# Block 2's gate and up projections in pairs of tiles by seven half-size products

## The chip, the cores and the metric

The kernel runs on one core of a Trainium2 chip. The metric is the device time of one execution in microseconds (us). All work is in float32. Matrix products that matter are made from float32r operands: each operand is split into a high half (rounded to float32r) and a low half (what is left), and three matmuls (high by high, high by low, low by high) are added in PSUM.

## The reference

Two transformer blocks of depth 2 on 512 tokens of width 1024. The part that the change touches is the feed-forward network of the second block, in both of its layers; it reads the whole token matrix `h` (512 x 1024):

```python
D_FF_2 = -(-(8 * D_MODEL) // (3 * 256)) * 256          # 2816
...
        h = h + mix @ w_out[l]
        hn = rms_norm_2(h, ffn_norm[l])
        gu = hn @ w_gate_up[l]
        h = h + (jax.nn.silu(gu[..., :D_FF_2]) * gu[..., D_FF_2:]) @ w_down[l]
```

## The kernel before

Activations lie feature-major: 128 features on the partitions, 512 tokens (`S`) in the free direction, so the width of 1024 is 8 k-tiles (`KD`) and the hidden width of 2816 is 22 tiles (`KF`). Weights come from HBM as units of 128 x 1024 float32 (512 KB): one unit holds the 8 k-tiles of one output tile. A ring of 4 units (`RING`) is filled by DMAs that SyncE issues (L425); a slot is filled again when `unit_free` says that its unit was split. For each unit ScalarE writes the high half into one of 2 slots (`SPLIT`) of `w_high` (L450) once TensorE is done with the unit two before (`split_used`), VectorE writes the low half into `w_low` (L453), and TensorE then does 8 k-tiles x 3 matmuls with it (L488), each 128x128 weights against 128x512 tokens.

The gate/up stage of block 2 has 22 output tiles of 2 units (gate, up). The tile's two products stand in banks 0 and 2 (or 4 and 6) of PSUM. The norm comes late: its gain is in the operand, and the reciprocal root of the mean square per token, `inv_rms`, is found during tile 0 (`LateNorm`: mean matmuls L560 on TensorE, root L1070 on ScalarE, three chained operations on VectorE, L783 to L785) and multiplied in when PSUM is read. Per tile (class `Swiglu`, scaled form): VectorE scales the gate (L1817) and the up part (L1818), ScalarE applies SiLU (L1801), VectorE multiplies (L1823), and the hidden tile is split for the down projection, high by ScalarE (L1789), low by VectorE (L1795), one tile later.

The down projection has 8 output tiles of 3 units (22 k-tiles). Its tile is added to the residual stream by VectorE (L1763), and the next norm's operand and squares are made tile by tile (L1024, L1029, L539). Its tile 0 waits for each hidden tile's halves, k by k.

Each engine's instructions are written out by hand in the order of its queue; semaphores alone tie the engines together. Nothing is planned by costs. `split_ahead` puts the next tile's unit splits ahead of the eviction of this tile on ScalarE and VectorE. `wait_tile` waits until the matmuls of a tile are done.

Of the kernel before, what the change touches and what calls it, by code (L numbers as in the profile page):

```python
# [22 lines left out]
ALU = mybir.AluOpType  # L23
# [21 lines left out]
RING = 4  # L45
SPLIT = 2
ADA_COLS = 256


Z_KA, Z_VA, Z_KB, Z_VB, Z_QA, Z_QB, Z_GA, Z_GB = 0, 1, 2, 3, 4, 8, 12, 20  # L50
# [19 lines left out]
def col_units(w):  # L70

    k, n = w.shape
    kt = k // P
    u = w.reshape(kt, P, n // P, P).transpose(2, 1, 0, 3).reshape(n // P, P, kt * P)
    pad = -u.shape[2] % UNIT
    if pad:
        u = np.concatenate([u, np.zeros((u.shape[0], P, pad), np.float32)], axis=2)
    return u.reshape(n // P, P, -1, UNIT).transpose(0, 2, 1, 3).reshape(-1, P, UNIT)


def modulation_units(w):
# [50 lines left out]
def weight_stream(a):  # L132
    out = []
    order = head_order()
    for l in range(DEPTH):
        qa, ka, va, qb, kb, vb, ga, gb = np.split(a["w_in"][l], np.cumsum([512, 128, 128, 512, 128, 128, D]), axis=1)
        keys, queries = pair_order(2), order[pair_order(8)]
        out.append(col_units(np.concatenate([ka[:, keys], va, kb[:, keys], vb, qa[:, queries], qb[:, queries], ga, gb], axis=1)))
        out.append(col_units(np.concatenate([a["w_proj_a"][l][order], a["w_proj_b"][l][order]], axis=0)))
        out.append(col_units(a["w_out"][l]))  # L140
        gate, up = col_units(a["w_ffn_gate"][l]), col_units(a["w_ffn_up"][l])
        out.append(np.stack([gate, up], axis=1).reshape(-1, P, UNIT))
        out.append(col_units(a["w_ffn_down"][l]))
    for l in range(DEPTH):
        w = a["w_in_2"][l]
        rope = np.concatenate([rope_order(w[:, 2560:], g) for g in range(4)], axis=1)
        out.append(col_units(np.concatenate([shift_order(w), w[:, SHIFTED * P:1920], rope, w[:, 1920:2560]], axis=1)))
        q_up = a["mla_w_q_up_2"][l].reshape(Q_RANK, HEADS, NOPE + ROPE)
        q_up = np.concatenate([rope_order(q_up[:, h, NOPE:], g) for g, h in enumerate(ROPE_HEADS)] +
                              [q_up[:, h, :NOPE] for h in range(HEADS)], axis=1)  # L150
        for k in range(Q_RANK // P):
            out.append(unit_of([(0, q_up[k * P:k * P + P])]))
        kv = a["mla_w_kv_up_2"][l].reshape(KV_RANK, HEADS, 2, HD)
        for part in range(2):
            m = kv[:, :, part].reshape(KV_RANK, HEADS * HD)
            out.append(unit_of([(0, m[:P]), (0, m[P:])]))
        out.append(col_units(a["w_out_2"][l]))
        gate, up = col_units(a["w_gate_up_2"][l][:, :DFF]), col_units(a["w_gate_up_2"][l][:, DFF:])
        out.append(np.stack([gate, up], axis=1).reshape(-1, P, UNIT))
        out.append(col_units(a["w_down_2"][l]))  # L160
    return np.concatenate(out)

# [145 lines left out]
def build(nc, dram, where, where1, where2, where3, n_units):  # L308
    with ExitStack() as ctx:
# [99 lines left out]
        def bank(n, w=BANK):  # L409
            return ps[:, n * BANK:n * BANK + w]  # L410
# [173 lines left out]
        def split_hidden(where_to):  # L584
# [17 lines left out]
            if where_to == "context":  # L602
                spans = [low[:, n:n + S] for n in range(KD * S, KD * T, S)]
                after = len(spans)
                spans += [m[:, n * S:n * S + S] for m, w in ((high, KD * T // S), (low, KD)) for n in range(w)]
            else:
                spans = [m[:, n * S:n * S + S] for m, w in ((high, KD * T // S), (low, KD)) for n in range(w)]
                spans += [low[:, n:n + S] for n in range(KD * S + 4 * C, KD * T, S)]
                after = KF
            return [[(hidL[:, k, :], spans[k], arena_r[:, k * S:k * S + S])] for k in range(KF)], after  # L610


# [1131 lines left out]
        class Residual(Evict):  # L1744


            def __init__(self, gate, later=None):
                self.gate, self.later = gate, later

            def scalar(self, act, g, t, c):  # L1750
                act.wait_ge(left_v.sem, left_v.at(t + 1))
# [6 lines left out]
            def vector(self, dve, g, t, c):  # L1758
                wait_tile(dve, g, t)
                for s, w in g.segs:  # L1760
                    x = (xL, xC)[s][:, t, :]
                    gate = 1.0 if self.gate is None else mod[:, self.gate + t, s:s + 1]
                    ins = dve.scalar_tensor_tensor(x, bank(4 * (c % 2) + s, w), gate, x, ALU.mult, ALU.add)  # L1763
                ins.then_inc(left_v.sem, 1)
                if self.later and t:
# [92 lines left out]
                        c.base += KF  # L1858

        gate_scaled, silu_out, hidden_out = (count(n) for n in ("gate_scaled", "silu_out", "hidden_out"))  # L1860
        first_root = arena[:, 21 * S:22 * S]

        def gemm(tiles, body, units, parts, segs, split, on_scalar=False):
# [1145 lines left out]
        for l in range(DEPTH):  # L3009
# [2 lines left out]
            mla(l)  # L3012
            inner_norm = late_norm("ffn", l, spare)
            next_norm = late_norm("attn", l + 1, spare) if l + 1 < DEPTH else None
            halves, after = split_hidden("alone")
            operand = [[(None, z2_r[:, HEADS + k if k < 4 else 2 * (k - 4), :], loL[:, k, :])] for k in range(KD)]
            stages = [Stage([gemm(KD, 4, 1, K8, segments(False), operand)], Residual(None, inner_norm), made=True)]
            stages += mlp(False, None, inner_norm, halves, after, None, next_norm)
# [49 lines left out]
```

## Time and profile before

| | |
|---|---|
| timed runs (3) | 3495.92, 3497.52, 3500.83 us; median 3497.52 |
| profiled execution, span | 3496.1 us |
| PE (TensorE matmul) busy | 3352.0 us, 96% |
| PEld (TensorE weight load) busy | 2656.6 us, 76% |
| DVE (VectorE) busy | 1643.4 us, 47% |
| ACT (ScalarE) busy | 1223.3 us, 35% |
| POOL (GpSimd) busy | 423.3 us, 12% |
| DMA | 82 GB/s in the mean |

Busy shares are means over the whole span. Rows of the trace give a start in us from the span's start, a duration, and behind them in brackets how long the engine sat idle before and which operation released it. A matmul's duration there is its latency; matmuls overlap, and their pace is read from one start to the next. The gate/up stage of block 2's first layer runs from about 2391 to 2649 us with the part of the stage before and behind it.

### The profile page before, as it was taken

Reading aid. Unit: us, or ns where it says so; the run is one execution under the profiler, and the core shown is the slowest. Engines: PE = TensorE matmul, PEld = TensorE weight load, DVE = VectorE, ACT = ScalarE, POOL = GpSimd, SP = SyncE. Lnnn points to the kernel's source line nnn. Section 1 sums busy time; section 2 is a strip of 40 time slices with the busy share of each in tenths; the row PEclk is TensorE's granted clock in tenths of the full one; section 3 lists DMA queues with packets and bytes.
Section 4 is the critical chain, followed back from the end, with each engine's and each line's share of the span. In section 5 each row is a group of like instructions: output and inputs, shape, how many; then the busy total and the mean of one; then the engine's idle time right before and its main releaser. Section 6 shows DMA issues by size and latency. Waiting matters only on the chain. (4 is left out here: it accounts for less than half of the span.)

```text
span 3496.1 us, 51241 instructions
## 1 busy us (share of the span) xinstructions
PE 3352.0 (96%) x21084; PEld 2656.6 (76%) x21084; DVE 1643.4 (47%) x2691; ACT 1223.3 (35%) x2135; POOL 423.3 (12%) x477
## 2 busy tenths in 40 slices
PE   6999999999999999999999999899999998999998
PEld 4887668788888787666787867657888777578886
DVE  4445754422132356665323347564443385744433
ACT  3215763321131222763223332353322332532322
POOL 0111110000000012112700133120000012210000
PEclk9999999999999999999999999999999999999999
DMA  5112331111212123322222322012222320022232
GB/s 210 61 60 99 109 122 66 50 66 61 67 61 73 55 79 101 129 70 97 90 91 91 105 89 67 20 37 92 96 95 98 102 85 9 31 91 95 92 99 82
DMA packets 89358, 287.61 MB, mean 82 GB/s; under 512 B 9904, under 2 KB 10288, under 8 KB 88752
## 3 DMA queue, kind: packets, MB, share of 16 engines
q1 hardware_dynamic: 89136, 284.41, 24.4%
q8 instruction: 168, 2.75, 0.3%
q14 instruction: 54, 0.44, 0.0%
HBM read 282.27 MB, written 2.10 MB: 81 GB/s over the span
## 5 line engine op out<-in xcount | busy, mean ns | idle before, releaser
L453 DVE TENSOR_TENSOR w_low<-ring,w_high 128x1024 fp32r<-128x1024 f32 x418 | 525.1, 1257 | 1523.2 <-ACT w_high L450 1522.6
L488 PE MATMUL ps<-arena_r,w_high 128*128 128x512 f32 x3568 | 1138.7, 384 | 10.1 <-PEq L1470 8.2
L450 ACT ACTIVATE w_high<-ring 128x1024 fp32r<-128x1024 f32 x418 | 442.8, 1060 | 1539.1 <-PE ps L488 1539.0
L488 PEld LDWEIGHTS ps<-arena_r,w_high 128*128 128x128 f32 x3568 | 646.1, 188 | 167.0 <-issue 15.6
L488 PE MATMUL ps<-low,w_high 128*128 128x512 f32 (+1 forms) x2448 | 765.0, 361 | 0.0
L488 PE MATMUL ps<-high,w_high 128*128 128x512 f32 x2368 | 735.8, 361 | 16.6 <-DVE low L947 8.6
L488 PE MATMUL ps<-high,w_low 128*128 128x512 f32 x2368 | 733.8, 360 | 0.0
L488 PE MATMUL ps<-arena_r,w_low 128*128 128x512 f32 (+1 forms) x1456 | 549.8, 390 | 0.0
L488 PEld LDWEIGHTS ps<-low,w_high 128*128 128x128 f32 x2448 | 410.8, 189 | 79.7 <-issue 1.1
L488 PEld LDWEIGHTS ps<-high,w_high 128*128 128x128 f32 x2368 | 394.2, 188 | 99.4 <-issue 12.2
L488 PEld LDWEIGHTS ps<-high,w_low 128*128 128x128 f32 x2368 | 393.7, 188 | 72.7
L488 PEld LDWEIGHTS ps<-arena_r,w_low 128*128 128x128 f32 x1456 | 267.0, 189 | 59.3
L549 POOL TENSOR_TENSOR tmp<-tmp 128x512 f32<-128x512 f32 (+1 forms) x42 | 60.9, 1451 | 1538.0 <-ACT tmp L539 1538.0
L1591 ACT ACTIVATE probs<-ps,stat 128x512 f32<-128x512 f32 (+3 forms) x224 | 153.0, 688 | 72.9 <-DVE stat L1549 34.8
L1488 PE MATMUL ps<-arena 64*128 64x256 f32 (+6 forms) x784 | 140.5, 431 | 19.0 <-ACT probs L1591 13.8
L1504 PE MATMUL ps<-const,probs 128*128 128x128 f32 x896 | 122.5, 279 | 15.8 <-DVE probs L1564 10.0
L1504 PEld LDWEIGHTS ps<-const,probs 128*128 128x128 f32 x896 | 98.2, 141 | 50.3 <-DVE probs L1564 39.4
L1582 ACT ACTIVATE probs<-ps 128x512 f32<-128x512 f32 (+3 forms) x224 | 120.8, 596 | 23.3 <-PE ps L1504 23.3
L488 PE MATMUL ps<-low,w_low 128*128 128x512 f32 x368 | 128.1, 376 | 0.0
L1488 PEld LDWEIGHTS ps<-arena 64*128 64x128 f32 (+1 forms) x784 | 79.2, 188 | 61.6 <-issue 32.5
L1517 PE MATMUL ps<-probs,arena 128*64 128x128 f32 x1792 | 123.0, 279 | 2.7 <-ACT hL L1603 1.3
L1517 PEld LDWEIGHTS ps<-probs,arena 128*64 128x64 f32 x1792 | 95.9, 137 | 38.4 <-issue 33.9
(359 smaller groups left out, 2866.0 us busy)
## 6 DMA issues: line engine op xcount, KB each, us to landing
ring<-in_weights SPq DMA_DIRECT2D x428, 512.0 KB, 3.4
hC<-in_ada SPq DMA_DIRECT2D x64, 256.0 KB, 3.0
high_f<-in_ada SPq DMA_DIRECT2D x40, 256.0 KB, 3.0
tmp<-in_ada SPq DMA_DIRECT2D x40, 256.0 KB, 3.5
arena<-in_ada SPq DMA_DIRECT2D x16, 512.0 KB, 15.6
arena<-in_ada SPq DMA_DIRECT2D x16, 256.0 KB, 4.0
xL<-in_x SPq DMA_DIRECT2D x1, 2048.0 KB, 10.0
out<-xL SPq DMA_DIRECT2D x4, 512.0 KB, 2.7
```

Source lines behind the costliest of these rows:

```text
L450: act.activation(w_high[:, slot, :], ring[:, place, :], ACT.Copy).then_inc(unit_high.sem, 1)
L453: dve.tensor_tensor(w_low[:, slot, :], ring[:, place, :], w_high[:, slot, :].bitcast(F32), ALU.subtract).then_inc(unit_free.sem, 1)
L488: mm = pe.matmul(bank(4 * (t % 2) + 2 * p + s, width), w, g.split[k][s][x], start=(n == 0 and m == 0), stop=(n == len(part) - 1 and m == 2))
L549: pool.tensor_tensor(tmp[:, 1, 0:total], tmp[:, 1, 0:total], tmp[:, 0, 0:total], ALU.add).then_inc(squares_sum.sem, 1)
L1488: mm = pe.matmul(ps[:, to:to + w], q, k, start=True, stop=True)
L1504: mm = pe.transpose(ps[:, to:to + P], probs[:, j % 3, e, m * P:m * P + P], con("ident"))
L1517: mm = pe.matmul(ps[e * HD:e * HD + HD, O_AT:O_AT + P], pair["values"][e][m], probs[:, j % 3, e, m * P:m * P + P], start=(m == 0 and not b ...
L1582: act.activation(probs[:, j % 3, e, 0:keys], ps[:, turned_at(j, e):turned_at(j, e) + keys], ACT.Copy).then_inc(turned_out.sem, 1)
L1591: act.activation(probs[:, i % 3, e, 0:keys], ps[:, scores_at(i, e):scores_at(i, e) + keys], ACT.Exp, bias=st[:, 2 + e:3 + e], scale=scale, ...
```

## The change

In block 2 the stage is rebuilt as class `SevenGates`. Its first two tiles (`DIRECT`) stay as before, except that the up part is no longer scaled. The other 20 tiles are done as ten pairs of tiles, and each pair in two steps: gate, then up. A step `w` takes two weight units (two output tiles) and sees the product as a 2x2 block product: output tiles 0 and 1; contraction halves of 4 k-tiles; token halves of 256 (`HALF`). It makes it from seven products of half-size operands, not eight (Strassen's scheme, in the form with common partial sums): A11, S1, S2, S3, A12, A22, S4, named by their weight operand. A product is 4 k-tiles x 3 matmuls of 128x128 weights against 128x256 tokens.

- Token operands that are sums (4 per contraction tile pair) are made once per layer, beside tiles 0 and 1: ScalarE scales the tokens, GpSimd makes the sums, ScalarE and VectorE split them (`blend_in`, `blended`, `blend_high`, `blend_low`).
- Weight operands that are sums (S1 to S4) are made for each step by VectorE from the ring (`sums_of`, 4 operations of 128x512), and all seven are split in halves of 128x512 (`hi_weights` on ScalarE, `lo_weights` on VectorE), four places in turn in `w_high` and `w_low`.
- The seven products share banks: 0, 1, 0, 2, 3, 2, 0 (or 4 more in odd steps). A12 has a bank of its own. S2 adds onto A11 after ScalarE has copied A11 out, A22 adds onto S3 after VectorE has read it, S4 adds nothing but needs bank 0 free.
- VectorE combines them with two copies in SBUF (5 operations of 128x256 per step), scales the gate pair after its step, and multiplies the pair after the up step. The up part's scaling by `inv_rms` moves behind the down projection (`Residual`, `scaled=True`): one more VectorE operation per down tile, in place in PSUM.
- Only the halves of hidden tiles 0 and 1 are made in the loop; 2 to 5 in the last step and 6 to 21 after it.
- The order of weight units in HBM is changed to fit (`gate_units`).

```diff
+            A11, S1, S2, S3, A12, A22, S4 = range(7)
+            SUMS = (S1, S2, S3, S4)
+            BANKS = (0, 1, 0, 2, 3, 2, 0)
+            FIRST = (0, 1, 3, 4, 6)
...
+            def tensor(self, pe):
+                g = self.gemms[0]
+                gemm_tensor(pe, g, (), self.normed)
+                for w in range(self.pairs):
+
+                    pe.wait_ge(left_v.sem, left_v.at(w + 1))
+                    for o in range(7):
+                        if o == self.S4:
+                            pe.wait_ge(unit_free.sem, self.unit(w + 1, 0))
+                        else:
+                            pe.wait_ge(half_low.sem, half_low.at(6 * w + o + 1))
+                        if o == self.S2:
+                            pe.wait_ge(copied.sem, copied.at(2 * w + 1))
+                        elif o == self.A22:
+                            pe.wait_ge(joined.sem, joined.at(4 * w + 2))
+                        elif o == self.S4:
+                            pe.wait_ge(copied.sem, copied.at(2 * w + 2))
+                        for j in range(4):
...
+                            for m, (weight, x) in enumerate(((hi_w, hi), (hi_w, lo), (lo_w, hi))):
+                                mm = pe.matmul(self.psum(w, o), weight, x, start=(o in self.FIRST and j == 0 and m == 0),
+                                               stop=(j == 3 and m == 2), skip_group_check=True)
...
+            def sums_of(self, dve, w, which):
+                a, b = (ring[:, self.unit(w, m) % RING, :] for m in range(2))
+                s1, s2, s3, s4 = self.s_f
+                steps = ((s1, b[:, 0:BANK], b[:, BANK:], ALU.add), (s2, s1, a[:, 0:BANK], ALU.subtract),
+                         (s3, a[:, 0:BANK], b[:, 0:BANK], ALU.subtract), (s4, s2, a[:, BANK:], ALU.subtract))
...
+            def scalar(self, act):
...
+                for w in range(self.pairs):
+                    last = w == self.pairs - 1
+                    for o, n in ((self.A11, 0), (self.S2, 1)):
+                        self.wait_product(act, w, o)
+                        if w >= 2:
+
+                            act.wait_ge(joined.sem, joined.at(4 * (w - 2) + 3 + n))
+                        act.activation(self.part[2 * (w % 2) + n], self.psum(w, o), ACT.Copy).then_inc(copied.sem, 1)
+                        if n == 0:
+                            self.hi_weights(act, w, 4)
+                            self.hi_weights(act, w, 5)
+                    self.hi_weights(act, w, 6)
+                    if w % 2:
+                        silu(DIRECT + w // 2, 2)
+                    if last:
+                        act.wait_ge(unit_free.sem, self.unit(w + 1, 0))
+                        for k in range(2, 6):
+                            self.high(act, k)
+                        self.ahead(act, None, 0)
+                        self.ahead(act, None, 1)
+                    else:
+                        for o in range(4):
+                            self.hi_weights(act, w + 1, o)
...
+            def vector(self, dve):
...
+                split_unit(None, dve, 2, 2, None, 0)
+                blend_lows(0)
+                blend_lows(1)
+                split_unit(None, dve, 3, 3, None, 0)
+                blend_lows(2)
+                self.normed.vector(dve)
+                blend_lows(3)
+                self.sums_of(dve, 0, range(4))
+                wait_tile(dve, g, 0)
+                scale(0, 1)
+                direct(0)
+                self.low(dve, 0)
+                self.lo_weights(dve, 0, 0)
+                self.lo_weights(dve, 0, 1)
+                wait_tile(dve, g, 1)
+                scale(1, 1)
+                self.lo_weights(dve, 0, 2)
+                self.lo_weights(dve, 0, 3)
+                direct(1)
+                self.low(dve, 1)
+                for w in range(self.pairs):
+                    last = w == self.pairs - 1
+                    p1, u2, u4 = self.part[2 * (w % 2)], self.part[2 * (w % 2) + 1], self.sum
+                    self.lo_weights(dve, w, 4)
+                    self.lo_weights(dve, w, 5)
+                    dve.wait_ge(copied.sem, copied.at(2 * w + 2))
+                    dve.tensor_tensor(u4, u2, self.psum(w, self.S1), ALU.subtract).then_inc(joined.sem, 1)
+                    self.lo_weights(dve, w, 6)
+                    if last:
+                        self.low(dve, 2)
+                        self.low(dve, 3)
+                    else:
+                        self.sums_of(dve, w + 1, (0, 1))
+                    self.wait_product(dve, w, self.S3)
+                    dve.wait_ge(joined.sem, joined.at(4 * w + 1))
+                    dve.tensor_tensor(self.result(w, 1, 1), u4, self.psum(w, self.S3), ALU.add).then_inc(joined.sem, 1)
...
```

In the two pieces below `[waits ...]` names the semaphores that an instruction waits for. First VectorE's queue in the middle of the stage before, two tiles of it (L453 weight low half, L1817 and L1818 scaling, L1795 hidden tile's low half, L1823 gate by up).

```order
1777 L1823 TENSOR_TENSOR arena<-arena,tmp 128x512 [waits left_psum_v,silu_out]
1778 L453 TENSOR_TENSOR w_low<-ring,w_high 128x1024 [waits unit_high] x2
1779 L1817 TENSOR_TENSOR tmp<-ps,inv_rms 128x512 [waits split_used]
1780 L1818 TENSOR_TENSOR arena<-ps,inv_rms 128x512
1781 L1795 TENSOR_TENSOR arena_r<-arena,high 128x512 [waits high_ready]
```

And VectorE's queue now, the body of one step (L2030 weight low half, L2006 weight sum of the next step, L2166 to L2192 combinations, of which L2175 reads S3).

```order
1814 L2030 TENSOR_TENSOR w_low<-ring,w_high 128x512 [waits half_high] x2
1815 L2166 TENSOR_TENSOR tmp<-const,ps 128x256 [waits copied]
1816 L2030 TENSOR_TENSOR w_low<-low_f,w_high 128x512 [waits unit_high]
1817 L2006 TENSOR_TENSOR low_f<-ring 128x512 [waits unit_landed1,unit_landed0]
1818 L2006 TENSOR_TENSOR low_f<-low_f,ring 128x512 [waits summed]
1819 L2175 TENSOR_TENSOR tmp<-tmp,ps 128x256 [waits joined,prod_done]
1820 L2179 TENSOR_TENSOR tmp<-const,ps 128x256 [waits prod_done]
1821 L2030 TENSOR_TENSOR w_low<-ring,w_high 128x512 [waits half_high]
1822 L2006 TENSOR_TENSOR low_f<-ring 128x512
1823 L2006 TENSOR_TENSOR low_f<-low_f,ring 128x512 [waits summed]
1824 L2186 TENSOR_TENSOR tmp<-const,ps 128x256 [waits prod_done]
1825 L2030 TENSOR_TENSOR w_low<-low_f,w_high 128x512 [waits half_high]
```

Two splits of 1024 and four operations of 512 per tile have become seven splits of 512, four sums, five combinations and two gate operations per step; between the combination of S1 and the reading of S3 stand S4's split and two of the next step's sums. On ScalarE the head of the stage now reads (L2059 wide high half of blended tokens, L459 unit split, L1078 the norm's root, L2064 SiLU, L2042 hidden tile's high half, L2019 weight half, L2094 copy of a product):

```order
1157 L2059 ACTIVATE high<-high_f 128x1024 [waits blended] x2
1158 L459 ACTIVATE w_high<-ring 128x1024 [waits split_used,unit_landed1]
1159 L2059 ACTIVATE high<-low_f 128x1024 [waits blended]
1160 L1078 ACT_TABLE_LOAD
1161 L1078 ACTIVATE inv_rms<-ps,eps 128x512 [waits pe_ready]
1162 L2059 ACTIVATE high<-low_f 128x1024 [waits blended]
1163 L2064 ACT_TABLE_LOAD
1164 L2064 ACTIVATE tmp<-tmp 128x512 [waits gate_scaled]
1165 L2042 ACTIVATE low<-arena 128x512 [waits left_psum_v]
1166 L2019 ACTIVATE w_high<-ring 128x512 [waits split_used,unit_landed2]
1167 L2019 ACTIVATE w_high<-low_f 128x512 [waits split_used,summed]
```

Three wide halves now stand ahead of the root or between it and the first SiLU, and the first product's halves stand behind tile 0's SiLU and hidden half.

## Rows read from the trace of the kernel before

**Rows 1.** The page's first part: busy us, share of span, instructions.
```profile
PE 3352.0 (96%) x21084; PEld 2656.6 (76%) x21084; DVE 1643.4 (47%) x2691; ACT 1223.3 (35%) x2135; POOL 423.3 (12%) x477
```
**Rows 2.** Window of the gate/up stage: busy PE, PEld, DVE, ACT, POOL; PEclk, DMA.
```profile
2405.00:2650.00 245.00, 245.00 (x1052) 197.10 (x1050) 105.08 (x129) 73.84 (x88) 0.00 (x0) 1.00 0.29 95
```
**Rows 3.** Timeline, DVE, same stage: start, us, engine, line.
```profile
2444.62 1.23 DVE L453 TENSOR_TENSOR w_low<-ring,w_high 128x1024 fp32r<-128x1024 f32 x1 [4.37 <-ACT w_high L450]
2445.76 0.68 DVE L1817 TENSOR_TENSOR tmp<-ps,inv_rms 128x512 f32<-128x512 f32 x1
...
2456.96 0.68 DVE L1817 TENSOR_TENSOR tmp<-ps,inv_rms 128x512 f32<-128x512 f32 x1
```
**Rows 4.** Timeline, PE and PEld, a stage of 512 and 256 columns in turn.
```profile
900.19 0.30 PEld L488 LDWEIGHTS ps<-low,w_high 128*128 128x128 f32 x2
...
900.30 0.51 PE L488 MATMUL ps<-low,w_high 128*128 128x512 f32 x2
900.65 0.51 PE L488 MATMUL ps<-high,w_low 128*128 128x512 f32 x2
```
**Rows 5.** Weight loads: by form (busy us, mean ns), and fp32 transposes' loads in time.
```profile
L488 PEld LDWEIGHTS ps<-arena_r,w_high 128*128 128x128 f32 x3568 | 646.1, 188 | 167.0 <-issue 15.6 <-DVE arena L2023 2.2 <-DVE arena_r L1029 0.7
...
2245.43 0.14 PEld L2765 LDWEIGHTS ps<-const,arena 128*128 128x128 f32 x1 [0.24 <-issue]
...
2245.86 0.80 PEld L2765 LDWEIGHTS ps<-const,arena 128*128 128x128 f32 x7 [0.29 <-issue]
```
**Rows 6.** Timeline: PE releases ACT; DVE releases PE.
```profile
240.05 0.51 PE L488 MATMUL ps<-high,w_low 128*128 128x512 f32 x2
...
240.66 1.06 ACT L450 ACTIVATE w_high<-ring 128x1024 fp32r<-128x1024 f32 x1 [6.28 <-PE ps L488]
...
1600.82 1.47 DVE L1719 TENSOR_TENSOR arena_r<-arena,high 128x512 fp32r<-128x512 f32 x2
...
1601.56 0.50 PE L488 MATMUL ps<-high,w_high 128*128 128x512 f32 x1 [0.80 <-DVE arena_r L1719]
...
1601.90 0.40 PE L488 MATMUL ps<-arena_r,w_high 128*128 128x512 f32 x1
```
**Rows 7.** ACT: by form (busy us, mean ns), and two in the timeline.
```profile
L1789 ACT ACTIVATE high<-arena 128x512 fp32r<-128x512 f32 x44 | 26.5, 625 | 30.2 <-DVE arena L1823 27.2 <-DVE arena L1828 3.0
...
L1807 ACT ACTIVATE tmp<-ps 128x256 f32<-128x256 f32 x22 | 8.3, 375 | 0.0
...
730.02 0.85 ACT L1807 ACTIVATE tmp<-ps 128x512 f32<-128x512 f32 x2
```
**Rows 8.** DVE: by form (busy us, mean ns), and two in the timeline.
```profile
L1795 DVE TENSOR_TENSOR arena_r<-arena,high 128x512 fp32r<-128x512 f32 x44 | 29.2, 684 | 1.8 <-ACT high L1789 1.8
...
L1828 DVE TENSOR_TENSOR arena<-tmp,ps 128x256 f32<-128x256 f32 x22 | 9.1, 412 | 0.0
...
731.29 1.01 DVE L1828 TENSOR_TENSOR arena<-tmp,ps 128x512 f32<-128x512 f32 x2
```
**Rows 9.** Timeline, ACT and DVE, the norm's root in this stage.
```profile
2397.01 1.06 ACT L450 ACTIVATE w_high<-ring 128x1024 fp32r<-128x1024 f32 x1 [4.54 <-PE ps L488]
2398.08 1.28 ACT L1070 ACT_TABLE_LOAD   x1
...
2399.38 0.69 ACT L1070 ACTIVATE inv_rms<-ps,eps 128x512 f32<-128x512 f32 x1
...
2400.84 0.70 DVE L784 SCALAR_TENSOR_TENSOR ps<-ps,inv_rms 128x512 f32<-128x512 f32 x1
2401.57 0.69 DVE L785 SCALAR_TENSOR_TENSOR inv_rms<-ps,inv_rms 128x512 f32<-128x512 f32 x1
```
**Rows 10.** By form (busy us, mean ns): a POOL and a DVE group.
```profile
L2529 POOL TENSOR_TENSOR work<-related,arena 128x256 f32<-128x256 f32 x40 | 26.0, 669 | 46.0 <-PE ps L2384 46.0
...
L1795 DVE TENSOR_TENSOR arena_r<-arena,low 128x512 fp32r<-128x512 f32 x38 | 26.8, 718 | 1.4 <-ACT low L1789 1.4
```
**Rows 11.** The page's DMA issues: KB each, median us to landing.
```profile
ring<-in_weights SPq DMA_DIRECT2D x428, 512.0 KB, 3.4
```

More of the change, by code:

```diff
@@ L47 @@
 ADA_COLS = 256
+HALF = 256
+DIRECT = 2
 Z_KA, Z_VA, Z_KB, Z_VB, Z_QA, Z_QB, Z_GA, Z_GB = 0, 1, 2, 3, 4, 8, 12, 20
@@ L78, in col_units, with gate_units @@
     return u.reshape(n // P, P, -1, UNIT).transpose(0, 2, 1, 3).reshape(-1, P, UNIT)
+def gate_units(gate, up):
+    first = [u[t] for t in range(DIRECT) for u in (gate, up)]
+    pairs = [u[t + m] for t in range(DIRECT, gate.shape[0], 2) for u in (gate, up) for m in range(2)]
+    return np.stack(first + pairs)
 def modulation_units(w):
@@ L158, in weight_stream @@
         gate, up = col_units(a["w_gate_up_2"][l][:, :DFF]), col_units(a["w_gate_up_2"][l][:, DFF:])
-        out.append(np.stack([gate, up], axis=1).reshape(-1, P, UNIT))
+        out.append(gate_units(gate, up))
         out.append(col_units(a["w_down_2"][l]))
@@ L606, in split_hidden @@
             else:
-                spans = [m[:, n * S:n * S + S] for m, w in ((high, KD * T // S), (low, KD)) for n in range(w)]
-                spans += [low[:, n:n + S] for n in range(KD * S + 4 * C, KD * T, S)]
-                after = KF
+                spans = [m[:, n * S:n * S + S] for m, ns in ((low, (10, 11, 4, 5, 6, 7)), (high, range(12)), (low, range(4))) for n in ns]
+                after = 2
             return [[(hidL[:, k, :], spans[k], arena_r[:, k * S:k * S + S])] for k in range(KF)], after
@@ L1744, in build, with __init__ @@
         class Residual(Evict):
-            def __init__(self, gate, later=None):
-                self.gate, self.later = gate, later
+            def __init__(self, gate, later=None, scaled=False):
+                self.gate, self.later, self.scaled = gate, later, scaled
             def scalar(self, act, g, t, c):
@@ L1762, in vector @@
                     gate = 1.0 if self.gate is None else mod[:, self.gate + t, s:s + 1]
+                    if self.scaled:
+                        chain_v.link(dve, dve.tensor_tensor(bank(4 * (c % 2)), bank(4 * (c % 2)), inv_rms[:, :], ALU.mult))
                     ins = dve.scalar_tensor_tensor(x, bank(4 * (c % 2) + s, w), gate, x, ALU.mult, ALU.add)
@@ L3014, in build @@
             next_norm = late_norm("attn", l + 1, spare) if l + 1 < DEPTH else None
-            halves, after = split_hidden("alone")
+            halves = split_hidden("seven")[0]
             operand = [[(None, z2_r[:, HEADS + k if k < 4 else 2 * (k - 4), :], loL[:, k, :])] for k in range(KD)]
             stages = [Stage([gemm(KD, 4, 1, K8, segments(False), operand)], Residual(None, inner_norm), made=True)]
-            stages += mlp(False, None, inner_norm, halves, after, None, next_norm)
+            stages.append(SevenGates(inner_norm, halves))
+            down = gemm(KD, 4, 3, [[(k // 8, k % 8, k) for k in range(KF)]], segments(False), halves)
+            stages.append(Stage([down], Residual(None, next_norm, scaled=True)))
             if next_norm:
```

205 lines of the change are left out of this document (added).

## The prediction

> **What bounds the kernel now.** I read the page's engine shares first, then the busy times of one gate/up stage by window, then the timeline of that stage, then single operations where the change needs a price. TensorE (PE) is busy 96% of the span [rows 1]. In the gate/up stage of block 2, layer 0, it is busy 245.00 us of 245, at a granted clock of 1.00 (the 2.4 GHz level), with VectorE (DVE) at 105 and ScalarE (ACT) at 74 [rows 2]. So nobody makes PE wait there, and the stage is worth its matmuls: VectorE's first operation of a tile starts every 11.20 us (2445.76 and 2456.96, [rows 3]), and a tile is two weight units of 24 matmuls, so a 512-column matmul takes 11.20 / 48 = 0.2333. 22 tiles make 246.4 us in each of the two layers. Only here does a removed matmul column pay at once; DVE has room for about as much work again, and that is the room the change spends.
>
> **Price of a 256-column matmul.** The trace has no run of fp32r matmuls that are all 256 wide, but it has them in turn with 512-wide ones: a couple starts every 0.35 us (900.30, 900.65, [rows 4]), so the narrow one takes 0.35 - 0.233 = 0.1167, exactly half. Each carries a full 128x128 weight load. Below: 0.110, the step of full-array fp32 loads in front of 128-column matmuls ((0.80 for seven - 0.14)/6, [rows 5]). Above: 0.188, if each load had to finish before its matmul [rows 5]. I take 0.1167, the nearest row, in which a full load already hides behind 256 columns.
>
> **Removed and added on PE.** A pair step (two weight units) was 48 x 0.2333 = 11.20 us. It becomes 7 products x 4 k-tiles x 3 = 84 matmuls x 0.1167 = 9.80 us. Twenty pair steps in each of two layers: 40 x -1.40 = **-56.0 us**. The first two tiles stay as they are.
>
> **The wait inside a pair step.** Products come in the order A11, S1, S2, S3, A12, A22, S4. A22 adds onto the bank in which S3 stands, so PE waits until DVE has read S3; and DVE has a queue ahead of that read. With T the start of the pair step:
> - S2's matmuls are streamed at T+4.20 (36 x 0.1167). ACT starts 0.38 after the start of the last 256-column matmul (240.28 to 240.66, [rows 6]): T+4.46.
> - ACT copies the product out, 0.375; its next instruction starts about 0.10 before an end (0.85 for a 512 and a 256 with 0.578 and 0.375, [rows 7]), so S4's high half runs from 4.74 to 5.37 (0.625, [rows 7]).
> - DVE waits for it and starts S4's low half at 5.40. A 512-wide DVE operation frees the engine after 0.60 and a 256-wide one after 0.33 (1.01 for two, less 0.412, [rows 8]); an operation that needs the one before starts 0.03 after its end, 0.715 in all (rows of chained steps, 0.73 for 0.70, [rows 9]). Low half 0.60, first sum of the next pair 0.715 (the second needs it), second sum 0.60: DVE reads S3 at 7.31 and is done at 7.73 (0.412, [rows 8]).
> - PE restarts 0.06 after the release, and its first matmul costs 0.11 more, the load being in the open (1600.82 + 0.684 to 1601.56; next start 1601.90, 0.34 later instead of 0.23, [rows 6]): in effect T+7.89, where it could have gone on at T+7.00.
>
> **0.89 us** per pair step; the step takes 10.69, not 9.80. 40 x 0.89 = **+35.6 us**. S3 and A12 lie inside this chain, so a step is 60 matmuls plus 3.69 us. S4's wait for its low half (done at 6.1) and the next A11's are met earlier.
>
> **Is DVE itself the bound?** Per pair step it issues 4 sums, 7 low halves, 2 gate operations (scaling in one step, product in the next), all 512 wide, and 5 combinations of 256: 13 x 0.60 + 2 x 0.115 + 5 x 0.33 = 9.68 us of 10.69. It fits, with 1 us to spare that its waits for ACT mostly take. ACT: 7 halves, 2 copies and a SiLU come to 5 us. POOL is idle in the loop. The weights: the ring's two slots of pair w-1 come free at 6.1 of that step, and DVE needs the units at 6.0 of the next, 10.6 us later; a unit lands 3.4 us after its issue [rows 11], two one behind the other 6.8.
>
> **Start of the stage**, per layer, counted from its first matmul. Tile 0 ends at 11.20, the mean's two matmuls, as today, at 12.1, tile 1 at 23.26. Beside them DVE now has four wide low halves of blended tokens (1.14 each, by 2444.62 to 2445.76, [rows 3]) and four sums (2.63). ACT can split the fourth direct unit only when the second's matmuls are done (11.5); its 0.95 and one wide blend (0.95) come before the reciprocal root, 1.28 for the table and 0.69 (to 15.3, [rows 9]); DVE then does the root's three steps (17.5), the last low half (18.6), the sums (21.3), scale, SiLU, product (each handing over to the other, 23.3), the hidden tile's halves and A11's (25.3). PE gets A11 at 25.5 instead of 23.3: **+2.25**. S2 then waits for ACT's copy, behind tile 1's scale, SiLU, product and high half: 30.7 instead of 28.3, **+2.41**. POOL's 16 blends of 256, 0.669 each with DVE quiet [rows 10], end near 13 and are not in this chain; their share of its cost I put at nothing, and if POOL were 2 us later ACT would still be at the root first.
>
> **End of the stage**, per layer. In the last step two low halves of hidden tiles stand where the sums stood, behind two SiLUs on ACT: 1.73 instead of 0.89, **+0.84**. The down projection's first unit can be split only when A22 is done with its slot (0.38 to ACT, 1.06, 1.23 [rows 3, 9] and the hops with the restart, 2.86 in all, against S4's 1.40): **+1.46**. The 16 low halves left over go at 0.60 each against PE's 0.70 per k; no wait. In sum 6.96 a layer, **+13.9 us**.
>
> **Down projection.** Its scaling by the root is one more DVE operation per tile. It hides behind 15.4 us tiles and, in layer 0, behind the 4.9 us that the next stage has before it needs the last k; only the very last is in the open: **+0.7 us**.
>
> **Sum**, against the profiled span of 3496.1: -56.0 + 35.6 + 13.9 + 0.7 = **-5.8**, hence 3490.3. The timed median, 3497.5, stands 1.4 above that span, and the same difference gives **3491.7 us**, 0.17% less. Seven eighths of the columns, and nearly all of the gain goes into waits. Each 0.1 us in the 3.69 moves the total 4 us, each ns of a narrow matmul 2.4 us (60 x 40), so 3484 to 3499 is this case's own range.
>
> **A rule that speaks against the change.** The load row is busy 197.10 of 245 us [rows 2], and the change makes 1056 loads a stage 1776; at 0.188 each [rows 5] these would be 334 us in a stage of 235. The Trainium skill ("Perfetto Trace Analysis", section "Identifying the Most-Contended Engine") says to judge TensorE's headroom by this share, loads' time over the window, and not by its matmuls'; by that the loads would be the bound. Against it: two full loads of 0.188 stood in 0.30 us [rows 4], the second 0.11 after the first, so their times overlap one another and their sum is no bound. It stays a rival, since no row has such loads for longer than a pair.
>
> **Rivals.**
> - *Loads bind (slower).* From the point where a load's own pitch exceeds 0.1167. At 0.125 a step is 60 x 0.0083 = 0.5 us longer: 3491.7 + 20 = 3512. At the full 0.188 it is 4.28 longer, near 3663. Chance 0.10, most of it at the lower end.
> - *DVE's queue is the bound (slower).* Place: the same A22 wait and the next step's gate operations. It decides once a 512-wide operation holds DVE for more than about 0.67: (10.69 - 1.65 - 0.23)/13. For: one group of 38 such operations had a mean of 0.718, not 0.684 [rows 10]; a wait may keep operations from overlapping. Then 13 x 0.684 + 5 x 0.412 = 10.9, with the 0.9 us of waits 11.8: 1.1 more, 3491.7 + 44 = 3536. Against: steps of 0.60 in two pairs of operations [rows 8]. Chance 0.09.
> - *The stream is faster.* At 0.110 a step is 0.40 shorter: 3476. For: [rows 5]; against: every 512-column fp32r matmul costs 0.2333, and the narrow one halves it exactly. Chance 0.08.
> - *The wait isn't there*, because DVE reads S3 before the sums or PE's queue covers it: 3491.7 - 35.6 = 3456. The order written out for DVE speaks against it. Chance 0.03.
>
> **Numbers.** Forecast 0.70, rivals 0.30. What this kernel's measurement can tell from no change is 0.2%, 7 us: faster is below 3490.5. The forecast's own 0.70 I split 0.27 faster, 0.40 same, 0.03 slower, since its centre is 1.2 us from the line but unpriced waits mostly add. With the rivals: faster 0.38, same 0.41, slower 0.21. The range 3478 to 3510 leaves out the far ends.
>
> **What would show it.** Per pair step (starts of the first product): 10.7 us; one PE wait of 0.8 to 1.0 us in each, before the sixth product, released by DVE's read of S3; narrow matmuls 0.117 apart; DVE busy above 90% in the loop and never long without work; two PE waits of some 2.3 us at the stage's start. Wrong, if the pitch of narrow matmuls is not 0.117, if PE waits elsewhere (for low halves, for weights), if the granted clock drops below 1.00 in the loop, or if DVE's 512-wide operations follow each other at more than 0.60.

## The result and the profile after

The changed kernel takes **3514.28 us** (median of 4 runs, 3513.11 to 3515.76), the kernel before 3496.72 beside it (3495.51 to 3500.83): ratio **1.0046**, 95% interval [1.0032, 1.0061]. It is slower by 17.6 us; 3491.7 was forecast. The profiled execution has a span of 3512.7 us at a granted clock of 0.989 (before: 3496.1 and 0.992).

Two lines of the profile after answer to [rows 1] and [rows 2]: the page's shares, and the busy times of PE, PEld, DVE, ACT and POOL in the gate/up stage.

```profile
PE 3320.7 (95%) x22524; PEld 2705.1 (77%) x22524; DVE 1897.1 (54%) x3231; ACT 1341.2 (38%) x2439; POOL 456.3 (13%) x509
...
2405.00:2650.00 245.00, 221.02 (x1736) 214.30 (x1735) 221.75 (x388) 125.84 (x230) 2.24 (x2) 0.99 0.27 92
```

PE was busy 245.00 of 245 us before; now it is without work for 24, and VectorE, at 105 before, is as busy as PE. What TensorE waits for in 2400 to 2650 (us in total, times, longest):

```profile
PE ps L1979 <- DVE w_low L2030: 7.8, 1, 7.8
PE ps L1979 <- DVE arena L2175: 7.4, 10, 1.4
PE ps L1979 <- DVE tmp L2175: 6.7, 10, 0.7
PE ps L497 <- DVE arena L2192: 1.5, 1, 1.5
PE ps L1979 <- ACT const L2094: 0.7, 1, 0.7
```

L1979 are the products' matmuls. One long wait stands before A11 (L2030, the weights' low half), one short wait in each pair step before A22 (L2175, VectorE's read of S3), one before the down projection.

A measure of the whole stage is the distance from VectorE's residual of the last out-projection tile to that of the first down tile. It takes layer 0 from 263.51 us (2388.05 to 2651.56) to 272.52 (2387.07 to 2659.59), and layer 1 by the same: 9.0 more in each. 0.72 of it is the new scaling ahead of that residual. All kernels below are measured so.

**Inside a pair step** the chain is as it was forecast (VectorE, then TensorE):

```profile
2500.84 0.42 DVE L2166 TENSOR_TENSOR tmp<-const,ps 128x256 f32<-128x256 f32 x1 [0.31 <-ACT const L2094]
2501.43 0.69 DVE L2030 TENSOR_TENSOR w_low<-low_f,w_high 128x512 fp32r<-128x512 f32 x1 [0.17 <-ACT w_high L2019]
2502.04 0.68 DVE L2006 TENSOR_TENSOR low_f<-ring 128x512 f32<-128x512 f32 x1
2502.76 0.69 DVE L2006 TENSOR_TENSOR low_f<-low_f,ring 128x512 f32<-128x512 f32 x1
2503.37 0.41 DVE L2175 TENSOR_TENSOR arena<-tmp,ps 128x256 f32<-128x256 f32 x1
```
```profile
2502.99 0.28 PE L1979 MATMUL ps<-arena_r,w_low 128*128 128x256 f32 x1
2503.93 0.48 PE L1979 MATMUL ps<-high,w_high 128*128 128x256 f32 x2 [0.66 <-DVE arena L2175]
```

S4's low half, two sums (L2006), then the read of S3, and TensorE goes on 0.15 behind its end. But a step is 10.97 us (2489.87 to 2500.84), not 10.69.

**At the head of the stage** A11 comes far later than forecast. TensorE (first the stage's first matmul, then the last of the direct tiles, A11 and S2):

```profile
2384.58 0.63 PE L497 MATMUL ps<-arena_r,w_high 128*128 128x512 f32 x2
...
2408.47 0.40 PE L497 MATMUL ps<-arena_r,w_low 128*128 128x512 f32 x1
2416.63 0.77 PE L1979 MATMUL ps<-arena_r,w_high 128*128 128x256 f32 x2 [7.76 <-DVE w_low L2030]
...
2421.88 0.47 PE L1979 MATMUL ps<-high,w_high 128*128 128x256 f32 x2 [0.74 <-ACT const L2094]
```

Counted from 2384.58, the turn of the direct tiles' last matmul ends at 2408.70, +24.1. The forecast had +23.26, because the mean's matmuls hold TensorE for 1.7 us and not 0.86; they do so in the kernel before too and cost nothing new. A11 stands at +32.05, not +25.5, and behind the end of the direct tiles 7.9 us and not 2.25: 5.7 more. ScalarE's queue shows why:

```profile
2398.45 1.06 ACT L2059 ACTIVATE high<-high_f 128x1024 fp32r<-128x1024 f32 x1 [2.61 <-POOL high_f L1992]
2399.42 1.04 ACT L459 ACTIVATE w_high<-ring 128x1024 fp32r<-128x1024 f32 x1
2403.34 1.06 ACT L2059 ACTIVATE high<-low_f 128x1024 fp32r<-128x1024 f32 x1 [2.88 <-POOL low_f L1992]
2404.42 1.28 ACT L1078 ACT_TABLE_LOAD   x1
2405.71 0.69 ACT L1078 ACTIVATE inv_rms<-ps,eps 128x512 f32<-128x512 f32 x1
```

The high halves (L2059) of the second and the third blend wait 2.61 and 2.88 us for GpSimd, and the root (L1078) stands behind both: it ends at +21.8, where the forecast had +15.3, 6.5 late like A11. The two waits are 5.5 of that. GpSimd's blends, and VectorE's wide operations at that time:

```profile
2399.20 0.74 POOL L1990 TENSOR_TENSOR low_f<-low_f 128x256 f32<-128x256 f32 x1
2400.02 1.61 POOL L1991 TENSOR_TENSOR low_f<-low_f 128x256 f32<-128x256 f32 x1
2401.71 1.60 POOL L1992 TENSOR_TENSOR low_f<-low_f 128x256 f32<-128x256 f32 x1
```
```profile
2399.55 1.48 DVE L2121 TENSOR_TENSOR high<-high_f,high 128x1024 fp32r<-128x1024 f32 x1 [1.72 <-ACT high L2059]
2400.95 1.76 DVE L462 TENSOR_TENSOR w_low<-ring,w_high 128x1024 fp32r<-128x1024 f32 x1
...
2408.63 1.23 DVE L2121 TENSOR_TENSOR low<-low_f,high 128x1024 fp32r<-128x1024 f32 x1
```

One operation of a blend takes 0.74 us alone (0.669 in [rows 10], another operation of the same size) and 1.60 beside a wide operation of VectorE, which itself goes from 1.23 to 1.48 or 1.76. The sixteen end at 2407.3, +22.7, where I had them near +13.

### The profile page after: what moved, and what is told of

Read it like the earlier page. It is cut to its first block and busy times, and to the rows that moved or that the text cites. A ratio compares the mean times of both kernels' runs of the same rounds, so it can differ in the third digit from the quotient of the medians.

```text
span 3512.7 us, 55491 instructions
## 1 busy us (share of the span) xinstructions
PE 3320.7 (95%) x22524; PEld 2705.1 (77%) x22524; DVE 1897.1 (54%) x3231; ACT 1341.2 (38%) x2439; POOL 456.3 (13%) x509
## 5 line engine op out<-in xcount | busy, mean ns | idle before, releaser
L462 DVE TENSOR_TENSOR w_low<-ring,w_high 128x1024 fp32r<-128x1024 f32 x338 | 428.3, 1267 | 1235.1 <-ACT w_high L459 1234.5
L459 ACT ACTIVATE w_high<-ring 128x1024 fp32r<-128x1024 f32 x338 | 357.9, 1059 | 1315.3 <-PE ps L497 1310.5
L497 PE MATMUL ps<-high,w_high 128*128 128x512 f32 x2368 | 738.5, 362 | 15.8 <-DVE low L955 8.0
L497 PE MATMUL ps<-arena_r,w_high 128*128 128x512 f32 x2288 | 739.0, 379 | 10.4 <-PEq L1478 8.2
L497 PEld LDWEIGHTS ps<-arena_r,w_high 128*128 128x128 f32 x2288 | 405.6, 188 | 107.4 <-issue 15.6
L497 PEld LDWEIGHTS ps<-high,w_high 128*128 128x128 f32 x2368 | 394.4, 188 | 97.3 <-issue 12.1
L497 PE MATMUL ps<-arena_r,w_low 128*128 128x512 f32 (+1 forms) x816 | 293.6, 382 | 0.0
L1979 PE MATMUL ps<-high,w_high 128*128 128x256 f32 x960 | 209.0, 286 | 28.9 <-DVE arena L2175 14.8
L1979 PE MATMUL ps<-arena_r,w_high 128*128 128x256 f32 x960 | 178.6, 284 | 15.5 <-DVE w_low L2030 15.5
L1979 PEld LDWEIGHTS ps<-high,w_high 128*128 128x128 f32 x960 | 159.9, 190 | 36.4 <-issue 36.4
L1979 PE MATMUL ps<-high,w_low 128*128 128x256 f32 x640 | 181.2, 283 | 0.0
L497 PEld LDWEIGHTS ps<-arena_r,w_low 128*128 128x128 f32 x816 | 146.3, 189 | 32.3
L1979 PEld LDWEIGHTS ps<-arena_r,w_high 128*128 128x128 f32 x960 | 150.1, 191 | 16.4 <-issue 16.4
```

What stands on the lines that cost most here:

```text
L459: act.activation(w_high[:, slot, :], ring[:, place, :], ACT.Copy).then_inc(unit_high.sem, 1)
L462: dve.tensor_tensor(w_low[:, slot, :], ring[:, place, :], w_high[:, slot, :].bitcast(F32), ALU.subtract).then_inc(unit_free.sem, 1)
L497: mm = pe.matmul(bank(4 * (t % 2) + 2 * p + s, width), w, g.split[k][s][x], start=(n == 0 and m == 0), stop=(n == len(part) - 1 and m == 2))
L1979: mm = pe.matmul(self.psum(w, o), weight, x, start=(o in self.FIRST and j == 0 and m == 0), stop=(j == 3 and m == 2), skip_group_check=True)
```

## The experiments

| kernel | us, median | ratio to before, interval | stage, layer 0 / 1, us |
|---|---|---|---|
| before | 3496.7 | | 263.51 / 263.52 |
| changed | 3514.3 | 1.0046 [1.0032, 1.0061] | 272.52 / 272.51 |
| e1_halves | 3509.95 | 1.0040 [1.0027, 1.0054] | 270.55 / 270.55 |
| e2_read_first | 3478.1 | 0.9950 [0.9937, 0.9964] | 253.80 / 253.78 |
| e3_root_first | 3508.3 | 1.0037 [1.0023, 1.0050] | 268.46 / 270.10 |
| e4_blends_dve | 3507.2 | 1.0038 [1.0024, 1.0051] | 269.91 / 269.52 |
| e5_dummies | 3518.1 | 1.0060 [1.0046, 1.0073] | 272.45 / 273.02 |
| e6_seven_head | 3459.9 | 0.9889 [0.9874, 0.9905] | 244.91 / 245.12 |
| e7_head_tail | 3462.4 | 0.9897 [0.9882, 0.9912] | 245.14 / 244.91 |
| e8_extra_op | 3486.7 | 0.9968 [0.9956, 0.9980] | 258.45 / 258.45 |
| e9_tail_order | 3457.6 | 0.9888 [0.9872, 0.9905] | 244.39 / 244.43 |

**e1_halves: the narrow matmul by itself.** It does not compute the reference's product (each half starts a sum of its own in the same bank); number, width and weights of its matmuls are those stated. `parts` is 2 in block 2's gate and up projections.

```diff
-                        mm = pe.matmul(bank(4 * (t % 2) + 2 * p + s, width), w, g.split[k][s][x],
...
+                        parts = 2 if g.halves else 1
+                        for h in range(parts):
+                            cols = slice(h * width // parts, (h + 1) * width // parts)
+                            mm = pe.matmul(bank(4 * (t % 2) + 2 * p + s, width)[:, cols], w, g.split[k][s][x][:, cols],
...
```


> The kernel before, with each 512-column matmul of block 2's gate and up projections issued as two of 256 columns on the same weights; the same columns, twice the matmuls and loads, nothing else moved. It measures the narrow matmul by itself. Theory (a narrow fp32r matmul costs 0.120, as it shows in the changed kernel, twelve per 1.44 us): a tile is 96 x 0.120 = 11.52 instead of 11.20 us, 44 tiles make +14 us, 3511. Rival 1 (it costs half of 0.2333, and the changed kernel's longer step comes from waits on VectorE): no change, 3497. Rival 2 (two loads of the same weights side by side cost more than in the pair step): tile of 12 us or more, 3532 or more.

A tile went to 11.52 us, by VectorE's first operation in each:

```profile
2448.57 0.68 DVE L1822 TENSOR_TENSOR tmp<-ps,inv_rms 128x512 f32<-128x512 f32 x1
...
2460.09 0.68 DVE L1822 TENSOR_TENSOR tmp<-ps,inv_rms 128x512 f32<-128x512 f32 x1
```

96 x 0.120 = 11.52; the stage is 7.04 longer, 22 tiles x 0.32. A narrow matmul among its like costs 0.120, as the theory had it. In the mixed stage of [rows 4] a narrow and a wide one together cost 0.350, which is less than 0.2333 + 0.120 = 0.3533. So the price depends on the company, and the forecast's row had the wrong one. That all of the difference falls to the narrow one there (0.1167) is a subtraction; no run shows how the two share it.

**e2_read_first: the wait before A22.**

```diff
                     self.lo_weights(dve, w, 6)
+                    self.wait_product(dve, w, self.S3)
+                    dve.wait_ge(joined.sem, joined.at(4 * w + 1))
+                    dve.tensor_tensor(self.result(w, 1, 1), u4, self.psum(w, self.S3), ALU.add).then_inc(joined.sem, 1)
                     ...
                         self.sums_of(dve, w + 1, (0, 1))
-                    self.wait_product(dve, w, self.S3)
-                    ...
```


> The changed kernel, with VectorE reading S3's product before it makes the next step's first two weight sums. Theory (the wait before A22 is VectorE's order and nothing else): VectorE reads S3 0.4 us after S3's last matmul, before TensorE is done with A12, the wait of 0.8 us in each pair step goes, and a step is 84 x 0.120 = 10.08 us: 40 steps by 0.9 less, 3478 to 3482. Rival (VectorE's queue is the bound, 10.1 us busy in a step of 11): the wait turns up elsewhere in the step, which stays above 10.5 us: 3495 or more.

Met: 36 us less than the changed kernel and 0.5% faster than before. What TensorE still waits for from 2400 to 2650, and the step, by VectorE's S2 combination:

```profile
PE ps L1979 <- DVE w_low L2030: 7.8, 1, 7.8
PE ps L497 <- DVE w_low L462: 1.4, 1, 1.4
PE ps L1979 <- ACT const L2094: 0.7, 1, 0.7
```
```profile
2483.35 0.42 DVE L2166 TENSOR_TENSOR tmp<-const,ps 128x256 f32<-128x256 f32 x1
...
2493.43 0.42 DVE L2166 TENSOR_TENSOR tmp<-const,ps 128x256 f32<-128x256 f32 x1
```

The twenty waits before A22 are gone, and a step is 10.08 us, 84 x 0.120. The order of two sums and one read had cost 18.7 us per layer.

**e3_root_first: the head's queue order.**

```diff
-                blend_highs(2)
                 self.normed.scalar(act)
-                blend_highs(3)
+                blend_highs(2)
                 silu(0, 1)
                 ...
+                blend_highs(3)
```

VectorE likewise: root, scaling, two sums, third low half, direct tile.


> The changed kernel, with the reciprocal root, the first tile's scaling and its SiLU taken ahead of the third and fourth blend on ScalarE and VectorE, and the sums for S3 and S4 after the first direct tile. Theory (A11 waits 7.8 us because the root stands behind GpSimd's blends in ScalarE's queue): TensorE's wait before A11 falls to about 1 us, a wait of about 2 us comes before S1 (fourth blend's low half), the granted clock stays above 0.5 in the head: 4 to 6 us less per layer, 3502 to 3506. Rival (all of the head's VectorE work is in the way, wherever the root stands): the waits only move from A11 to S1 and S2, under 2 us gained per layer, 3510 or more.

6 us less in all: more than the rival's, less than the theory's 8 to 12. In both layers A11 waits 2.36 us, S1 0.23, and S2 3.05 (for ScalarE's copy, behind the second tile's SiLU and high half), which I had not priced; so part of the gain moved to S2. Layer 0 gains 4.1 us and layer 1 only 2.4, and the clock is the difference. In layer 0 the granted clock stays at 1.00. In layer 1 the same three waits are followed by a clock of 0.50 (the lower level, 1.2 GHz) from about 3144 to 3151:

```profile
3145.38 0.77 PE L1979 MATMUL ps<-high,w_high 128*128 128x256 f32 x2 [3.06 <-ACT const L2094]
...
3146.00:3147.00 1.00, 1.00 (x6) 1.00 (x6) 1.00 (x2) 0.27 (x1) 0.00 (x0) 0.50 0.00 0
```

Nobody makes TensorE wait behind S2's start there, so the slow matmuls count in full: from S2's start to A22's it takes 6.88 us, against 5.22 in layer 0, and 1.64 is what layer 1 lost.

**e4_blends_dve: who makes the blends.**

```diff
-                    chain_g.link(pool, pool.tensor_tensor(x11, x11, x12, ALU.subtract))
-                    ...
+                chain_v.link(dve, dve.tensor_tensor(x11, x11, x12, ALU.subtract))
+                ...
```


> The changed kernel, with the blends of the tokens made by VectorE (two column groups at a time, eight operations of 512 elements) instead of GpSimd (sixteen of 256). Theory (GpSimd is late because its operations and VectorE's wide ones lengthen each other): the wide low halves fall from 1.48 to 1.76 back to 1.14 to 1.23 us, ScalarE no longer waits for blends, and A11 starts 3 us earlier in each layer although VectorE has 5.6 us more to do: 3506 to 3509. Rival (VectorE's total work in the head is the bound): A11 is as late or later, 3514 to 3524.

Met: with GpSimd out, all wide low halves are back at 1.2 us each, and the stage is 2.6 and 3.0 us shorter although VectorE has eight operations of 0.69 more. ScalarE waits for one blend still, 1.31 us for the third, instead of 2.61 and 2.88 for two.

```profile
2398.01 2.35 DVE L2125 TENSOR_TENSOR high<-high_f,high 128x1024 fp32r<-128x1024 f32 x2
2400.28 1.22 DVE L462 TENSOR_TENSOR w_low<-ring,w_high 128x1024 fp32r<-128x1024 f32 x1
2401.41 1.22 DVE L2125 TENSOR_TENSOR low<-low_f,high 128x1024 fp32r<-128x1024 f32 x1
```

A11 still waits 4.80 us: VectorE's own order (both last low halves and four sums ahead of the scaling) is next.

**e5_dummies: does the slow clock cost anything?** In the changed kernel the granted clock falls while TensorE has no work, and A11 and the first matmuls of S1 run at the lower level, 1.2 GHz (time window, PE busy, PEld, DVE, ACT, POOL, clock):

```profile
2412.00:2413.00 1.00, 0.00 (x0) 0.00 (x0) 1.00 (x2) 0.00 (x0) 0.00 (x0) 0.98 0.00 0
2414.00:2415.00 1.00, 0.00 (x0) 0.00 (x0) 0.50 (x1) 0.47 (x1) 0.00 (x0) 0.50 0.00 0
2418.00:2419.00 1.00, 1.00 (x7) 1.00 (x6) 0.09 (x1) 1.00 (x3) 0.00 (x0) 0.50 0.06 16
2420.00:2421.00 1.00, 1.00 (x10) 0.93 (x8) 0.80 (x2) 0.17 (x1) 0.00 (x0) 1.00 0.00 0
```
```diff
                 gemm_tensor(pe, g, (), self.normed)
+                x = g.split[0][0][1]
+                for _ in range(28):
+                    pe.matmul(bank(1), x[:, 0:P], x, start=True, stop=True, skip_group_check=True)
```


> The changed kernel, with 28 matmuls of 512 columns (tokens against tokens, 6.5 us, into a bank that A12's predecessors don't read) issued between the two direct tiles and A11, in TensorE's 7.8 us without work; nothing else waits for them. Theory (the idle stretch costs twice: the wait itself, and 1.7 us more because A11 and S1 run at a granted clock of 0.50): A11 starts when it did, the clock stays at 1.00, its 24 matmuls take 2.9 us instead of 4.6: 1.6 us less per layer, 3511. Rival (the clock falls whatever TensorE does there, from what the other engines do): no change, 3514; or A11 itself was held by the slow clock: no change either.

The theory was wrong, and the rival's "no change" came for another reason than its two. In layer 0 A11 started when it did (32.06 behind the stage's first matmul), the clock stayed at 1.00, and A11 and S1 took 2.9 us, but S2 then waited longer:

```profile
2417.86 0.48 PE L1982 MATMUL ps<-arena_r,w_high 128*128 128x256 f32 x2 [1.41 <-DVE w_low L2033]
...
2423.11 0.47 PE L1982 MATMUL ps<-high,w_high 128*128 128x256 f32 x2 [2.13 <-ACT const L2097]
```

S2 starts 5.25 us behind A11 in both kernels (2416.63 to 2421.88, and 2417.86 to 2423.11): ScalarE's queue sets it, and the half clock lay inside that wait at no cost. Layer 1 begins the same way, but there the clock falls to 0.50 from about 3156.3 to 3159.7, in S2 and S3, behind S2's wait of 2.15; its first step takes 11.39 us instead of 10.98. So a slow clock is free only where another queue sets the next start. That the median is 3.8 us above the changed kernel's is not explained by the stages (272.45 and 273.02); the two intervals overlap.

**e6_seven_head: the head in the order that TensorE needs.** The early read and the blends on VectorE, and in the head (VectorE's part):

```diff
+                self.sums_of(dve, 0, (0, 1))
+                self.blends(dve, 0)
                 split_unit(None, dve, 2, 2, None, 0)
-                blend_lows(0)
-                blend_lows(1)
+                self.blends(dve, 1)
                 split_unit(None, dve, 3, 3, None, 0)
-                blend_lows(2)
                 self.normed.vector(dve)
-                blend_lows(3)
-                self.sums_of(dve, 0, range(4))
                 wait_tile(dve, g, 0)
                 scale(0, 1)
+                self.sums_of(dve, 0, (2, 3))
                 direct(0)
+                blend_lows(0)
                 self.low(dve, 0)
                 self.lo_weights(dve, 0, 0)
+                blend_lows(1)
                 self.lo_weights(dve, 0, 1)
+                blend_lows(2)
+                blend_lows(3)
...
```

The second direct tile follows; its SiLU and its halves lie inside the first pair step.


> The changed kernel with VectorE's early read of S3, the blends on VectorE, the first two weight sums made while ScalarE still scales the tokens, the root, scaling and SiLU of the first direct tile ahead of the wide low halves, these and the low halves of the weights in the order in which TensorE asks for them, and the second direct tile's SiLU and halves inside the first pair step. Theory (the head's miss is order and contention, and VectorE has just time for all of it): the wait before A11 and before S2 fall from 8.5 to under 1 us per layer and the clock stays at 1.00: 9 us less per layer than with the early read alone (3478): 3460. Rival (VectorE's total in the head is the bound, whatever the order): a wait of 3 us or more comes back at S1 or S2: 3467 or more.

Met. A11 follows the direct tiles without a gap, the granted clock stays at 1.00 in both heads, and what is left in layer 0's head is one wait of 0.6 us in the first pair step:

```profile
2410.01 0.39 PE L497 MATMUL ps<-arena_r,w_low 128*128 128x512 f32 x1
2410.24 0.40 PE L1979 MATMUL ps<-arena_r,w_high 128*128 128x256 f32 x2
```

8.9 and 8.7 us less per layer than e2, and **1.1% faster than before**.

**e7_head_tail and e9_tail_order: the wait before the down projection.** e7 splits the first down unit in two halves, the first when A12's half slot is free:

```diff
+                    for m, o in enumerate((self.A12, self.A22)):
+                        part = slice(m * BANK, m * BANK + BANK)
...
+                            self.wait_product(act, last, o)
+                            ins = act.activation(w_high[:, slot, part], ring[:, place, part], ACT.Copy)
...
```


> The kernel just described, with the down projection's first weight unit split in two halves, the first as soon as A12's slot half is free, the second after A22. Theory: the wait of 1.4 us before the down projection falls to about 0.3: 2 us less in both layers together, 3458. Rival (ScalarE's or VectorE's queue at the stage's end holds the second half up): no difference.

The rival was right: no gain, 3462.4 against 3459.9. VectorE's tile halves (L2051) kept the first half (L2072) back until the second was ready too:

```profile
2612.57 0.69 DVE L2051 TENSOR_TENSOR arena_r<-arena,low 128x512 fp32r<-128x512 f32 x1
2613.17 0.41 DVE L2215 TENSOR_TENSOR arena<-const,ps 128x256 f32<-128x256 f32 x1
2613.50 1.28 DVE L2072 TENSOR_TENSOR w_low<-ring,w_high 128x512 fp32r<-128x512 f32 x2
```

e9 moves tiles 4 and 5 behind the unit in both queues.

```diff
-                        self.low(dve, 4)
                     self.wait_product(dve, w, self.A12)
                     ...
-                        self.low(dve, 5)
+                        self.ahead(None, dve, 0, (0,))
```


> The kernel with the down projection's first weight unit split in two halves, now with both engines' queues at the stage's end in the order that this needs: ScalarE takes the two halves ahead of the hidden tiles 4 and 5, VectorE the first low half right behind its read of A12 and the second behind A22, tiles 4 and 5 after S4. Theory (in the version before, VectorE's low halves of tiles 2 to 5 stood ahead of the first half's, so that both came back to back): TensorE's wait before the down projection falls from 1.4 to 0.5 us or less; the two layers together gain about 2 us on the kernel with the rewritten head (3459.9): 3458. Rival (the unit's last half, ScalarE 0.6 and VectorE 0.7 behind A22, is itself as long as S4's cover): the wait stays above 1 us, 3460.

The wait fell from 1.36 to 0.22 us; the stage gained 0.5 and 0.7 on e6, since about half came back, in layer 0 as two small gaps in the first down tile (0.5 with their restarts). 3457.6 against 3459.9 are within each other's spread; the shorter stage is seen in both layers.

**e8_extra_op: how near is VectorE to the bound?** e2 with one more operation per step:

```diff
+                    more = inv_rms[:, :].rearrange("p (a c) -> p a c", a=2)
+                    dve.tensor_tensor(ps[:, :].rearrange("p (b c) -> p b c", b=8)[:, 4 * (w % 2) + 2:4 * (w % 2) + 4, HALF:], more, more, ALU.mult)
```


> The changed kernel with VectorE's early read of S3, and one more 512-element operation of VectorE at the end of each pair step, which nobody waits for. Theory (with the wait gone, TensorE's 10.08 us bound the step with VectorE at 9.7 close behind): the queue now needs 10.3 us and more: a step grows by 0.2 to 0.6, 40 of them make +9 to +24, 3487 to 3502. Rival (VectorE's busy time overstates its load and it has 1 us to spare): 3478 to 3480.

8.6 us more, the lower edge of the theory's range. The step is VectorE's queue, without a gap: 10.33 us.

```profile
2488.66 0.41 DVE L2166 TENSOR_TENSOR tmp<-const,ps 128x256 f32<-128x256 f32 x1
...
2498.99 0.41 DVE L2166 TENSOR_TENSOR tmp<-const,ps 128x256 f32<-128x256 f32 x1
```

So the forecast's 9.68 us of VectorE per step was sound (9.68 + 0.60 = 10.28), and the fixed kernel has 0.4 us of it left.

## Why the prediction was wrong

Right were the pair step's chain and its place (e2 took it away: 0.89 us per step, 10.97 to 10.08, as priced; both the chain and the matmuls that it covers were 0.08 longer), VectorE's load (e8), the tail's place, the down scaling's 0.7 (0.73 at the very end), and that loads of 0.188 each do not bind by their sum. S2's start behind A11 (5.25 against 5.2) was right partly by luck, since A11 ran at half the clock assumed and the queue hid it. Of the 11.5 us per layer that the stage is longer than forecast:

- **The head, 5.7.** This step failed: "POOL's 16 blends [...] end near 13, and are not in this chain". The price 0.669 came from a row with VectorE quiet [rows 10], and the sentence said so, but here VectorE's widest operations run beside. Five of the sixteen took 1.60 instead of 0.74, 4.3 us in all; where nothing disturbed them they stood 0.82 and not 0.669 apart, about 2.0; and the first began 3.5 later than I had it (+5.8 and not +2.3), when ScalarE had its tokens ready. The cover that I gave, "if POOL were 2 us later ACT would still be at the root first", was 2 us against 9.7, and the root, on which the whole chain to A11 hangs, stands behind the second and the third blend's high halves in ScalarE's queue, which waited 5.5 us for GpSimd. Of the 6.5 by which A11 was late, 0.86 lay under the mean's matmuls, which I had at half their time; 5.7 are left. e3 and e4 each take back a part, e6 all of it. That two engines lengthen each other I had left out; the Trainium skill ("SBUF — State Buffer", section "Who interferes with whom") says that a VectorE instruction with two SBUF inputs contends with a GpSimd instruction that reads SBUF. This trace agrees (0.74 to 1.60, 1.23 to 1.76), and e4 removes both.
- **The step's length, 5.3** (0.28 x 19). 0.20 of each is the narrow matmul, 60 x 0.0033 (e1); 0.08 is the chain, 3.77 us and not 3.69. The step's form, 60 matmuls plus a chain, held; the term was mis-sized because the row chosen mixed widths. The rival "loads bind" named the right term, with a pitch of 0.125 beyond the 0.120 measured; that the loads are what sets 0.120 is not shown. Its far end was worked out too low: 84 loads of 0.188 are 15.8 us, 5.1 above the step of 10.69 and not 4.28.
- **The last step and the tail, 0.5 together.** The last step 11.73 against 11.53, A22 to the down projection 4.56 against 4.27.

5.7 + 5.3 + 0.5 = 11.5 per layer, 23.0 in all, of the 23.4 between the forecast change (-5.8) and the measured one (+17.6). No rival put anything into the head, and the range up to 3510 had no term for it, because POOL's blends had been given no upper bound.

Not settled: why narrow matmuls cost 0.0033 more among their like (e1 shows only that they do), and why in e3 the clock fell in layer 1 and not in layer 0 behind the same waits.

## What to carry to other kernels

A scheme that trades matmuls for vector work is decided by the order in the vector queues: here the same 84 matmuls made the kernel 0.5% slower or 1.1% faster. Ask of each wait what stands in front of the releasing instruction but isn't needed by it, and put reads that free a bank ahead of work for the next step. A duration taken from a quiet engine needs an upper bound wherever two engines will run side by side, above all when the chain to TensorE's next start is queued behind it.

## What was not expected of the hardware

- GpSimd and VectorE lengthen each other's SBUF operations: 0.74 to 1.60 us (128x256) and 1.23 to 1.76 (128x1024) in the changed kernel's head; with GpSimd out (e4) the latter are back at 1.2.
- A 256-column fp32r matmul costs 0.120 us in a row of such, and a couple with a 512-column one 0.350, 0.0033 less than the two prices (0.120 and 0.2333) add up to.
- The granted clock fell to 0.50 behind idle stretches of 4.8 us (e4) and 7.8 us of TensorE. Behind waits of 2.4, 0.2 and 3.05 us it stayed at 1.00 in one layer and fell to 0.50 in the other (e3).
- A fallen clock cost nothing where another engine's queue set the next start (e5, layer 0), and 1.6 us where TensorE's own pace did (e3, layer 1).
